# A decoder trunk on one core: output projection and feed-forward as one block, with the norm's root factor applied after the products

## What is computed

```python
def rmsnorm(x, g, eps=1e-6):
    xf = x.astype(jnp.float32)
    y = xf * lax.rsqrt(jnp.mean(xf * xf, axis=-1, keepdims=True) + eps)
    return (y * g.astype(jnp.float32)).astype(x.dtype)

def swiglu(x, wg, wu, wd):
    return (jax.nn.silu(x @ wg) * (x @ wu)) @ wd
...
        y_p = y_p + mix_p
        y_s = y_s + mix_s
        y_p = y_p + swiglu(rmsnorm(y_p, norm_ffn[layer]), ffn_gate[layer], ffn_up[layer], ffn_down[layer])
        y_s = y_s + swiglu(rmsnorm(y_s, norm_ffn[layer]), ffn_gate[layer], ffn_up[layer], ffn_down[layer])
```

## Time and profile before

| | |
|---|---|
| Median of 3 runs | 4461.98 us (4452.33 to 4477.48) |
| Profiled execution | 4452.25 us, its span 4450.4 us |
| TensorE busy, share of the span | 3873.8 us, 87% |
| DVE, ACT, POOL busy | 1361.1 (31%), 795.4 (18%), 481.8 us (11%) |
| Output projection, layers 0 and 1 | 1801.6 to 1899.7 us, 3462.7 to 3561.2 us |
| First feed-forward product, layers 0 and 1 | 1958.3 us, 3618.4 us |

### The profile page before, as it was taken

The page is one execution under the profiler, slowest core; times in us unless marked ns, Lnnn a source line. Parts: engine busy times, 40 slices in busy tenths (PEclk is TensorE's granted clock), DMA queues, the critical chain, the costliest instruction groups (busy, mean ns, idle before and its releaser), DMA issues. The chain is left out here.

```text
span 4450.4 us, 62608 instructions
## 1 busy us (share of the span) xinstructions
PE 3873.8 (87%) x26171; PEld 3226.1 (72%) x26171; DVE 1361.1 (31%) x2514; ACT 795.4 (18%) x1483; POOL 481.8 (11%) x342
## 2 busy tenths in 40 slices
PE   6698988869778856869999999999996869999996
PEld 4467767734445633859999998576675859999996
DVE  2344534422256622232112123223223132112211
ACT  1122220101045600121111111112111121111110
POOL 0000000000400000112122221000000112222221
PEclk9799998889879965989999999999995989999998
DMA  2000000010400021111111110201112111111112
GB/s 86 13 11 16 21 6 11 7 71 20 112 24 1 6 75 46 58 36 49 40 41 52 38 43 31 93 15 59 40 40 86 63 39 51 39 42 47 39 42 91
DMA packets 75722, 189.10 MB, mean 42 GB/s; under 512 B 30836, under 2 KB 45108, under 8 KB 72260
## 3 DMA queue, kind: packets, MB, share of 16 engines
q1 hardware_dynamic: 62724, 157.97, 10.8%
q0 software_dynamic: 8448, 27.27, 1.9%
q10 hardware_dynamic: 4352, 1.05, 0.2%
HBM read 161.34 MB, written 29.04 MB: 43 GB/s over the span
## 5 line engine op out<-in xcount | busy, mean ns | idle before, releaser
L392 DVE TENSOR_TENSOR ff_prod<-ff_silu,ps 128x384 f32<-128x384 f32 x132 | 62.4, 528 | 874.0 <-PE ps L234 874.0
L234 PE MATMUL ps<-ffn_high,ff_gh 128*128 128x384 f32 (+1 forms) x1056 | 234.7, 330 | 71.9 <-POOL ff_gl L276 71.9
L2323 PE MATMUL ps<-act,gl_w 128*128 128x384 f32 (+1 forms) x768 | 243.3, 477 | 0.0
L234 PE MATMUL ps<-ff_hh,ff_dh 128*128 128x384 f32 (+1 forms) x1056 | 233.2, 328 | 4.6 <-DVE ff_hl L397 4.6
L234 PEld LDWEIGHTS ps<-ffn_high,ff_gh 128*128 128x128 f32 x1056 | 181.9, 189 | 72.9 <-POOL ff_gl L276 72.9
L234 PE MATMUL ps<-ffn_high,ff_gl 128*128 128x384 f32 (+1 forms) x1056 | 234.1, 330 | 0.0
L234 PE MATMUL ps<-ffn_low,ff_gh 128*128 128x384 f32 (+1 forms) x1056 | 234.0, 329 | 0.0
L234 PE MATMUL ps<-ffn_high,ff_ul 128*128 128x384 f32 (+1 forms) x1056 | 232.7, 328 | 0.0
L234 PE MATMUL ps<-ffn_low,ff_uh 128*128 128x384 f32 (+1 forms) x1056 | 232.7, 328 | 0.0
L234 PE MATMUL ps<-ffn_high,ff_uh 128*128 128x384 f32 (+1 forms) x1056 | 232.7, 328 | 0.0
L234 PE MATMUL ps<-ff_hh,ff_dl 128*128 128x384 f32 (+1 forms) x1056 | 232.7, 328 | 0.0
(11 more groups left out here) (562 smaller groups left out, 7069.8 us busy)
## 6 DMA issues: line engine op xcount, KB each, us to landing
ff_wg<-in_wg SPq DMA_DIRECT2D x44, 512.0 KB, 3.6
ff_wu<-in_wu SPq DMA_DIRECT2D x44, 512.0 KB, 3.6
ff_wd<-in_wd POOLq DMA_DIRECT2D x48, 256.0 KB, 3.0
ff_wd<-in_wd POOLq DMA_DIRECT2D x32, 320.0 KB, 3.4
ns_past<-in_cache_slc SPq DMA_DIRECT2D x64, 128.0 KB, 2.0
rw_w<-in_w_rwkv SPq DMA_DIRECT2D x14, 512.0 KB, 3.6
np_w<-in_w_nsa SPq DMA_DIRECT2D x2, 2608.0 KB, 11.8
resid<-in_x SPq DMA_DIRECT2D x1, 4352.0 KB
```

The lines of the kernel that those rows point to most:

```text
L234: mm = pe.matmul(g.ps[:, bank + c, 0:n], w[:, k, :], x[:, kx, o:o + n], start=(first and i == 0), stop=(last and i == 2))
L392: m = dve.tensor_tensor(prod[:, o:o + n], silu[:, o:o + n], g.ps[:, 3 + c, 0:n], ALU.mult)
L2323: mm = pe.matmul(out[:, 0:n], w[:, k, :], g.act[:, k, o:o + n], start=(k == 0), stop=(k == KT - 1))
```

## The change

The three blocks become one, `output_and_feed_forward`. The norm is taken apart. The feed-forward multiplies the residual times the gain only; the root factor of each token, which is the same for all channels, is applied after the products: once to the gate's PSUM before Silu, and once to Silu's result, where it stands for the factor of the up product.

- While the output tiles run, ACT makes for each finished tile t the rounded `resid * gain` (`fh`) and the square of the tile, DVE the low rest (`fl`), and POOL adds the squares up over the tiles (`sqsum`).
- TensorE makes three matmuls on `sqsum` (banks 6, 7) inside the first gate pass; ACT takes the root and DVE the reciprocal under the products.
- In each hidden tile DVE reads the gate's PSUM times `rs` into `silu`, ACT applies Silu there in one instruction, and DVE multiplies by `rs` again.
- The weight buffers of both phases are one pair, `w`, `wh`, `wl`, so the first gate and up weights are loaded behind the last output weights. The wait before the first down weight's load is for the last output tile. The 8 output tiles are straight code now, and so is the first gate and up pass.

Core of the diff:

```diff
+            def add_squares(t):
+                norm.squared.next(pool)
+                if t >= 1:
+                    pool.drain()
+                    pool.tensor_tensor(sqsum, sqsum, sq, ALU.add).then_inc(norm.summed.sem, 1)
...
+            for t in range(KT):
+                if t + 2 < KT:
+                    low_out(t + 2)
+                if t == KT - 2:
+                    low_gate(F0)
+                add_squares(t)
...
+            def sums(c):
+                o, n = CH[c]
+                pe.matmul(g.ps[:, 6 + c % 2, 0:n], g.mean[:, :], sqsum[:, o:o + n], start=True, stop=True).then_inc(norm.mean_ready.sem, 1)
+
+            def gate(f, opening=False):
+                pe.wait_ge(s.gate_lo, f + 1)
+                pe.wait_ge(s.gate_out, f + 1)
+                for k in range(KT):
+                    if opening:
+                        pe.wait_ge(norm.lowered.sem, T0 + k + 1)
+                    mm = products(pe, g, 0, wh[0], wl[0], k, fh[k], fl[k], k == 0, k == KT - 1)
+                    if opening and k == KT - 3:
+                        pe.wait_ge(norm.summed.sem, (layer + 1) * (KT - 1))
+                        sums(0)
+                        sums(1)
+                mm.then_inc(s.gate_done, 1)
+                if opening:
+                    pe.wait_ge(norm.root_ready.sem, 3 * g.norms + 1)
+                    sums(2)
...
+            def gained(t):
+                act.wait_ge(so.out, T0 + t + 3)
+                norm.rounded.mark(act.activation(fh[t][:, :], g.resid[:, t, :], ACT.Copy, scale=gain[:, t:t + 1]))
+                if t >= 2:
+                    act.wait_ge(norm.summed.sem, layer * (KT - 1) + t - 1)
+                norm.squared.mark(act.activation(sqsum if t == 0 else sq, g.resid[:, t, :], ACT.Square))
...
             def swish(f):
-                act.wait_ge(s.gate_done, f + 1)
-                act.wait_ge(s.up_out, f + 1)
-                for c, (o, n) in enumerate(CH):
-                    a = act.activation(silu[:, o:o + n], g.ps[:, c, 0:n], ACT.Silu)
-                a.then_inc(s.gate_out, 1)
...
+                act.wait_ge(s.gate_out, f + 2)
+                act.activation(silu[:, :], silu[:, :], ACT.Silu).then_inc(s.silu_done, 1)
...
+            for t in range(KT):
+                if t + 2 < KT:
+                    high_out(t + 2)
+                if t == KT - 2:
+                    act.wait_ge(so.done, T0 + KT - 1)
+                    high_gate(F0)
+                gained(t)
+            act.wait_ge(so.done, T0 + KT)
             high_up(F0)
+            for c in range(3):
+                root(c)
...
-                    dve.wait_ge(s.gate_out, f + 2)
+                    dve.wait_ge(s.gate_done, f + 1)
+                    for c, (o, n) in enumerate(CH):
+                        m = dve.tensor_tensor(silu[:, o:o + n], rs[:, o:o + n], g.ps[:, c, 0:n], ALU.mult)
+                    m.then_inc(s.gate_out, 1)
+                    dve.wait_ge(s.silu_done, f + 1)
+                    dve.tensor_tensor(silu[:, :], silu[:, :], rs, ALU.mult)
+                    dve.drain()
                     dve.wait_ge(s.up_done, f + 1)
```

More of the change, by code:

```diff
@@ L189, in square @@
                 o, n = CH[c]
-                s.squared.mark(act.activation(sq[:, c % 2, :, 0:n], g.resid[:, :, o:o + n], ACT.Square))
+                s.squares.mark(act.activation(sq[:, c % 2, :, 0:n], g.resid[:, :, o:o + n], ACT.Square))
             square(0)
@@ L217, in _, with products @@
                 for k in range(KT):
[L218 to L224, removed]
-def products(pe, g, bank, hi, lo, k, xh, xl, kx, first, last):
+                    dve.scalar_tensor_tensor(out[:, k, o:o + n], g.resid[:, k, o:o + n], gain[:, k:k + 1], rs[:, c, 0:n], ALU.mult, ALU.mult)
+def products(pe, g, bank, hi, lo, k, xh, xl, first, last):
     passes = ((hi, xh), (lo, xh), (hi, xl))
@@ L305, in _, with up @@
         def _(pe):
+            def sums(c):
[16 more added lines that the diff above has]
+                    sums(2)
+            def up(f, n0):
+                pe.wait_ge(s.up_lo, f + 1)
+                pe.wait_ge(s.up_out, f + 1)
+                pe.wait_ge(s.down_out, n0 + 2)
+                for k in range(KT):
+                    mm = products(pe, g, 3, wh[1], wl[1], k, fh[k], fl[k], k == 0, k == KT - 1)
+                mm.then_inc(s.up_done, 1)
+            for t in range(KT):
+                pe.wait_ge(so.lo, T0 + t + 1)
+                pe.wait_ge(so.out, T0 + t + 1)
+                for k in range(KT):
+                    if t == 0:
+                        split.both.next(pe)
+                    mm = products(pe, g, 3 * (t % 2), wh[t % 2], wl[t % 2], k, ah[:, k, :], al[:, k, :], k == 0, k == KT - 1)
+                mm.then_inc(so.done, 1)
             for part, (f0, nf) in enumerate(PARTS):
@@ L382, in _ @@
             if layer == 0:
+                dve.sem_inc(so.out, 2)
+                dve.sem_inc(s.gate_out, 1)
                 dve.sem_inc(s.up_out, 1)
                 dve.sem_inc(s.down_out, 2)
+            for k in range(KT):
+                split.high.next(dve)
+                split.both.mark(dve.tensor_tensor(al[:, k, :], act_in[:, k, :], ah[:, k, :].bitcast(F32), ALU.subtract))
+            for t in range(KT):
+                dve.wait_ge(so.done, T0 + t + 1)
+                for c, (o, n) in enumerate(CH):
+                    m = dve.tensor_tensor(g.resid[:, t, o:o + n], g.resid[:, t, o:o + n], g.ps[:, 3 * (t % 2) + c, 0:n], ALU.add)
+                m.then_inc(so.out, 1)
+                norm.rounded.next(dve)
+                norm.lowered.mark(dve.scalar_tensor_tensor(fl[t][:, :], g.resid[:, t, :], gain[:, t:t + 1], fh[t][:, :].bitcast(F32),
+                                                           ALU.mult, ALU.subtract))
+            for c, (o, n) in enumerate(CH):
+                dve.wait_ge(norm.root_ready.sem, 3 * g.norms + c + 1)
+                dve.reciprocal(rs[:, o:o + n], rs[:, o:o + n])
+            dve.drain()
             for part, (f0, nf) in enumerate(PARTS):
```

234 lines of the change are left out of this document (95 added, 139 removed).

## The result

| | before | after |
|---|---|---|
| Median of the timed runs, us | 4458.48 (4 runs, 4452.33 to 4477.48) | 4345.62 (4 runs, 4338.90 to 4349.36) |
| Profiled execution, us | 4452.25 | 4342.08 |
| Ratio, with its 95% interval | | 0.9738 [0.9713, 0.9762] |

Faster by 2.6%, and 5.6 us above the forecast of 4340. The comparison was made twice more: 0.9720 [0.9704, 0.9737] with a median of 4334.58, and 0.9721 [0.9694, 0.9748] with 4340.36.

The account below looks back on a forecast made before the run. TensorE, busy 87% of the span, was taken as the bound. Seams of 58.72 + 57.36 us and 4.26 of cold restart go, 3.65 return: 4452.25 - 116.7 = 4335.6, with half the median's excess 4340 us; range 4322 to 4360.

Parts of the forecast that it names:

- Saved, less the sums, both layers: Seams between output projection and feed-forward: 120.3 us go, 3.65 us return for six matmuls on the summed squares, leaving 116.7.
- E: The end of output tile 7, from which the prediction counts times at the joint; tile 6 ended at E - 12.
- POOL's last addition done, asked for: At the joint, POOL's last addition of squares takes 2.6 us, done E + 6.5; TensorE asks at E + 9.
- Second gate weights ready, wanted: Longest new chain at the joint: weights ready E + 24.1, wanted E + 25.8; margin 1.7 us, the thinnest.
- Chain per tile: In 44 feed-forward tiles, gate pass end to next gate weights: 6.3 us, 6.6 with collision, against the up pass's 12.
- The main term: TensorE goes straight from output tile 7 into the first gate tile: 58.72 + 57.36 + 4.26 = 120.3 us saved, before sums.
- The signs: New profile: no PE idle over 1 us from output tiles to first up pass, 24.0 us per tile, clock 1.00.
- The bound on the reciprocal: Root chain at the joint: reciprocal taken as free beside POOL, or blocked by two down-weight splits of 1.5 us, 3.0 us.
- The collisions: DVE and POOL refusing each other SBUF access: at most one full operation, 2.6 us, per collision; 0.3 us at k = 7.
- A late root chain: Rival, chance 0.12: seam closes but root chain comes 3 to 10 us late per layer; gain 97 to 111, 4346 to 4360.
- the steady chain: Rival, chance 0.02, slower or no gain: per-tile gate chain becomes the bound; each us beyond 12 costs 44, break-even 14.7.
- the level: Timed median lay 9.7 us above the profiled execution; half of such an excess was taken, lifting 4335.6 to 4340 us.

## Why the prediction was right

| Step | forecast | measured |
|---|---|---|
| Saved, less the sums, both layers | 116.7 us | 116.1 us between the marks |
| Sums, per layer | 1.83 us | 1.81 us |
| Up pass starts | E + 13.8 | E + 13.4 |
| Low part of k = 7 ready | E + 4.1 | E + 4.1 |
| POOL's last addition done, asked for | E + 6.5, E + 9 | E + 6.5, E + 8.8 |
| Reciprocals end | E + 17.7 | E + 17.3 |
| Second gate weights ready, wanted | E + 24.1, E + 25.8 | E + 23.7, E + 25.6 |
| Chain per tile | 6.3 or 6.6 us | 6.2 us |
| Gate or up pass in the steady state | 12.0 us | 12.0 us |

**The main term was right, and for its reason.** Seam, cold restart and sums add up to the trace's difference, and the experiment that normalises first, which keeps the joint block, loses 23.3 us a layer. That the two agree within 0.6 us is in part luck, since the measured difference is 114.1 to 116.4 us depending on the pair of profiles. The signs held as well: no idle time between the output tiles and the first up pass, 24.0 us per tile, granted clock 1.00 from 3509.7 to 4307. Only "first gate pass about 13.2 us" does not fit the prediction's own sum of 12 + 1.83; it took 13.55 (1905.93 to 1919.48).

**The bound on the reciprocal is closed, but the reason given was too narrow.** The prediction took the reciprocal as free beside POOL, since it has one SBUF input, and kept 3.0 us as a bound. In the seam above DVE's three reciprocals run without a gap from 1916.37 to 1923.34 (6.97 us, where one over all 1088 elements takes 6.95), while POOL's two subtractions run from 1921.16 in 3.09 us, near the 1.5 each of the estimate by size. Neither held the other up. One SBUF input alone does not make an instruction free, though: the cast has one, and goes from 0.73 to 2.53 us beside POOL. The Trainium skill (SBUF — State Buffer, section SBUF: two separate sides) gives the shared pair to a DVE instruction with two SBUF inputs or one in a 2-port mode, and the prediction left out the second case. The trace agrees with the page for the subtraction and the reciprocal; that the cast runs in such a mode isn't shown by it.

**The collisions came, and were hidden.** The source line of the low part, in ns (least, median, most), shows that 14 of 16 were slowed:

```profile
L487 DVE SCALAR_TENSOR_TENSOR ff_x<-resid,param,ff_x x14: 2008/2064/2145, 1824.8 to 3500.6; 128x1088 fp32r<-128x1088 f32 x14
L487 DVE SCALAR_TENSOR_TENSOR ff_x_low<-resid,param,ff_x x2: 1351/1352/1352, 1908.8 to 3512.6; 128x1088 fp32r<-128x1088 f32 x2
```

```profile
L301 POOL TENSOR_TENSOR ff_stats<-ff_stats x14: 2612/3328/3393, 1838.0 to 3513.7; 128x1088 f32<-128x1088 f32 x14
```

At tiles 0 to 6 DVE takes 0.7 us longer, and at tiles 1 to 6 POOL's addition too, under 12 us of products each. In one such tile DVE's subtraction starts at 1836.82, while POOL's weight split runs until 1837.82, and ends 1.15 us behind that; POOL's addition starts at 1837.98 and ends 2.40 us behind DVE's end at 1838.97. So each loses about what was left of the other's operation, 0.7 us here, far from the 2.6 that the prediction set as the most. At tile 7, where it would count, they overlap by 0.2 us (1909.95 to 1910.17), where the prediction had 0.3, and both keep their time. In the steady tiles DVE's second multiplication runs into POOL's weight split, which takes 2.55 us there and 2.41 for the up weights.

**Two prices in the rivals were off.** A late root chain was counted one to one (3 to 10 us late, 6 to 20 us lost). The runs show a step beside the slope: 4.85 us of wait cost 7.4 and 6.55 cost 8.9, some 2.3 to 2.5 us of half clock each, and even 1.85 us cost 3.7, while about 1 us of wait in every tile left the granted clock at 1.00. By that step the rival's upper end would be 4365 and not 4360. And the steady chain was to cost 44 us for each us over 12; only 34 tiles can wait for it (34 waits over both layers with 6.95 us added). By that count its break-even is estimated at 12 + 116.7 / 34 = 15.4 us in place of 14.7.

**What it missed by 5.6 us** is the level, not the change. The prediction set the level by half of the 9.7 us between the profiled run and the median. The first 1800 us wander by more: the first output product stood at 1801.7 and 1803.9 us in two profiles of before, at 1807.8, 1813.5 and 1806.8 in three of after, and from 1802.1 to 1821.2 in the six experiments that change nothing ahead of it. Eight of these nine profiles of the new code lie behind both of before, which speaks for a lasting cost of some us. Two things speak against it. The medians are 112.9, 125.7 and 121.3 us apart in the three comparisons, mean 120, and the interval of the second, 117 to 132 us, has no room for a gain of 116 less 6. And the difference arises in one stage, the sparse attention over the cached tokens, where before's own two profiles part as well, by the clock (last section). So it isn't settled whether the changed kernel loses a few us there.

## What to carry over

A factor that is the same for all channels of a token commutes with the product: take it out of the operand and apply it where PSUM is read anyway, and the reduction that makes it can run under the first products. Price such a change by the marks on TensorE (last product before, first product after), lay the new chain out step by step against the moment at which its result is asked for, and look up the thinnest margin first: here 2.0 us, and 2.1 and 2.3 by lengthening the chain until TensorE waited. A chain that overruns its margin costs half clock on top of the wait. Count the places that can wait, not the tiles. When a gap is closed, look at the next one up the same queue: here a load that was issued behind others had 14 us in it for the two layers.

## What the runs showed of the hardware

- **One wait of 2 us in a full stream already costs more than itself.** Behind single waits of 1.85, 4.85, 6.55 and 11.45 us came products at half clock (group to group up to 1.08 us in place of 0.50), which cost 1.6, 2.4, 2.5 and 1.4 us on top. So the extra cost did not grow with the wait in these runs. Waits of 1.03 us, 16 of them in a layer, left the clock full.
- **Products in float32 between products in fp32r** cost their own time and no more: 0.99 + 0.28 us for two sums of 384 tokens, 0.54 for one of 320.
- **The same code at the same moment ran at either clock.** Up to the sparse attention over the cached tokens the two profiles of before lie 0.6 us apart (DVE's copy in L1019 starts at 1553.85 and 1553.26). Then these products of before's first profile ran at full clock and those of its second at half:

```profile
1559.37 1.45 PE L1097 MATMUL ps<-ns_past,ns_qs 64*32 64x512 f32 x3
```

```profile
1559.37 2.76 PE L1097 MATMUL ps<-ns_past,ns_qs 64*32 64x512 f32 x3
```

DVE's next mark, L1167, comes at 1568.78 in the first and at 1576.32 in the second, and the copy in L1231 at 1594.90 and 1605.51. By the first output product 8 of these 11 us have come back. Ten of the thirteen profiles of this study, before's second among them, took 8 to 11 us longer from the mark in L1019 to the one in L1167 than before's first. Why the clock falls in one execution and not in another isn't shown by these runs; it is the reason for reading an effect of a few us between marks inside the stage, and not in the total.
